# One decoder step: in the chunked recurrence, half of the heads keep their token rows in the other half of the partitions, and the products between channels and tokens are issued in turn through four quarters of TensorE

## The chip, the core and the metric

The kernel runs on one NeuronCore of one Trainium2 chip. The metric is the device time of one execution in microseconds. A core has TensorE (PE in the rows, with its weight loads apart as PEld), VectorE (DVE), ScalarE (ACT), GpSimd (POOL) and SyncE (SP), each with its own instruction stream; they wait for one another through semaphores. TensorE's results land in PSUM, which has 128 partitions and eight banks; everything else is held in SBUF, with 128 partitions too.

## The reference

One inference step of a decoder layer is computed for a prompt of 1024 tokens and for 8 samples of 4 new tokens. The layer has an input projection, an RWKV7 recurrence beside latent attention, a memory attention and a convolutional feed-forward part. Only the recurrence concerns us. For each of 8 heads a 64 x 64 state S is carried over the tokens:

```python
def step(S, inp):
    r_t, d_t, k_t, v_t, kk_t, a_t = inp
    sa = -jnp.einsum('bhvk,bhk->bhv', S, kk_t)
    S = (S * d_t[:, :, None, :] + sa[..., None] * (kk_t * a_t)[:, :, None, :]
         + v_t[..., None] * k_t[:, :, None, :])
    return S, jnp.einsum('bhvk,bhk->bhv', S, r_t)
...
state, out = lax.scan(step, state0.astype(jnp.float32), xs)
```

## The kernel before

**Layout.** The recurrence is `rwkv_chunk_stage` (from L1756). The 1024 prompt tokens are cut into 16 chunks of 64 tokens (`NCH` is 16, `CH` is 64), and a seventeenth pass does the 32 sample tokens in the same way. Eight heads are four pairs p: pair p has one head's 64 channels in partitions 0 to 63 and the other's in 64 to 127 (`HALF`). Pairs 0 and 1 form half `hf` 0, pairs 2 and 3 half 1, and each half has four PSUM banks of its own: PX, PY, PV and PU.

**Quarters.** Every matmul of this stage has a 64 x 64 float32 stationary operand. The partitions it reads decide which 64 rows of TensorE's array it uses, and the partitions of its output decide which 64 columns. Before the change a head's token rows lie in the same half of the partitions as its channels, so each product reads and writes one half: only two of the array's four quarters are used, rows 0 to 63 with columns 0 to 63 and rows 64 to 127 with columns 64 to 127. A float32 matmul appears in the trace as two MATMUL records (passes), each with a weight load. In the program a loop over `HALF` issues the two heads of a pair one after the other.

**One chunk c, in TensorE's order** (rows' names in brackets):

1. `pe_products(c)`: the products of keys and queries (rc_KR, rc_BK; L1805 with 128 moving columns, L1808), which fire `a_made` for each half, and transposes by the identity (L1816), which fire `vt_made` for each half.
2. `solution(c-1)`: L2010 and L2012 accumulate the right-hand side of the previous chunk in PU and fire `sa_made`.
3. `pe_first_level(c)`: L1830, L1832, L1834.
4. `outputs(c-1)`: state and output of the previous chunk, five products for each pair (L2022, L2024, L2026, L2028, L2030), which fire `o_made`.
5. `pe_levels(c)`: levels 1 to 5 of a triangular inverse by repeated squaring (L1847, L1850, L1853), the two halves in turn, and then L1859.

**VectorE for the same chunk:** `dve_masks(c)` (L1937, L1939, L1944 for each half, after `a_made`; the second fires `a_taken`), `dve_solution(c-1)` (L1965 for each half), `dve_state(c-1)` (L1972 twice and L1974 for each half, after `o_made`), then `dve_levels(c)` (L1955 for each level and half, which fires `t_taken`, with the operands of the next chunk, L1917 to L1928, between levels). **ScalarE** copies PY to SBUF after `vt_made` (L1881), copies the levels' results (L1890, L1893, L1895), L1905 for rc_WT (`wt_taken`), and scales the old state (L2050). Each engine runs its list in that order; a product of level n+1 waits for VectorE's `t_taken` and ScalarE's `n_taken` of level n for its half.

Of the kernel before, what the change touches and what calls it, by code (L numbers as in the profile page):

```python
# [18 lines left out]
ALU = mybir.AluOpType  # L19
# [17 lines left out]
CH = 64  # L37
NCH = TP // CH
# [93 lines left out]
class K:  # L132
# [74 lines left out]
class TokenScale:  # L207
# [4 lines left out]
    W = C3 // 4  # L212
# [1540 lines left out]
HALF = slice(0, HD), slice(HD, P)  # L1753


def rwkv_chunk_stage(k, c, b, kk, keep, free_b, free_kk, tail, mh_at):  # L1756


# [5 lines left out]
    S = {n: k.sem(f"rc_{n}") for n in (  # L1764
        "masks", "zero", "prev", "exp", "bd", "a_made", "vt_made", "a_taken", "l_taken", "vt_taken",
        "lev_made", "n_taken", "t_taken", "mv_taken", "wt_made", "wt_taken", "sa_made", "sa_taken",
        "o_made", "o_taken", "end", "s1", "s_ready", "out",
        "ut_made", "ut_taken", "m_own", "sb_in", "sx_made", "sx_taken", "ex", "ns_made", "sum", "ns_done")}
    NT_, N_, TT_ = 0, 1, 2

# [2 lines left out]
    PX, PY, PV, PU = [[k.bank[4 * hf + n] for hf in range(2)] for n in range(4)]  # L1773
    two = lambda bank, lo, w=CH: bank[:, lo:lo + 2 * w].rearrange("p (q n) -> p q n", q=2)
    at = lambda n, w=CH: slice(n, n + w)
    L_RAW, MV_, WT_, SA_, ST_, O_ = 128, 256, 384, 0, 128, 256
    ident = [k.masks[h, MK["ident"] + j * HD:MK["ident"] + (j + 1) * HD] for j, h in enumerate(HALF)]
    with ExitStack() as ctx:
        rm = k.sb(ctx, "rc_masks", [P, 2, 4, CH])
# [16 lines left out]
        def pe_products(pe, c_):  # L1796

            sl = c_ % 2
            KR, BK = KR_[:, sl], BK_[:, sl]
            pe.wait_ge(S["bd"], 5 * (c_ + 1))  # L1800
            for hf in range(2):
                for q, p in enumerate(pairs(hf)):
                    for j in range(2):
                        for h in HALF:
                            pe.matmul(PX[hf][h, at(256 * q + 128 * j, 128)], BK[h, p, j, :],  # L1805
                                      KR[h, p].rearrange("p a n -> p (a n)"), start=True, stop=True)
                    for h in HALF:
                        mm = pe.matmul(PV[hf][h, at(L_RAW + 64 * q)], KR[h, p, 0, :], BK[h, p, 0, :], start=True, stop=True)  # L1808
                mm.then_inc(S["a_made"], 1)
            for hf in range(2):  # L1810
                if c_:
                    pe.wait_ge(S["wt_taken"], 2 * (c_ - 1) + hf + 1)
                for q, p in enumerate(pairs(hf)):
                    for j in range(4):
                        for i, h in enumerate(HALF):
                            mm = pe.matmul(PY[hf][h, at(256 * q + 64 * j)], BK[h, p, j, :] if j < 3 else KR[h, p, 0, :], ident[i],  # L1816
                                           start=True, stop=True)
                mm.then_inc(S["vt_made"], 1)

        def pe_first_level(pe, c_, levels):  # L1820
            W, A4, tm = W_[:, c_ % 2], A4_[:, c_ % 2], tm_[:, c_ % 2]
# [15 lines left out]
        def pe_levels(pe, c_, levels):  # L1837
            W, tm = W_[:, c_ % 2], tm_[:, c_ % 2]
            for lev in range(1, levels):
                for hf in range(2):  # L1840
                    if lev == 1:
                        pe.wait_ge(S["mv_taken"], 2 * c_ + hf + 1)
                    pe.wait_ge(S["n_taken"], 10 * c_ + 2 * (lev - 1) + hf + 1)
                    pe.wait_ge(S["t_taken"], 12 * c_ + 2 * (lev - 1) + hf + 1)
                    for q, p in enumerate(pairs(hf)):
                        for h in HALF:
                            mm = pe.matmul(PV[hf][h, at(64 * q)], W[h, p, N_, :], W[h, p, TT_, :], start=True, stop=True)  # L1847
                        if lev < levels - 2:
                            for h in HALF:
                                pe.matmul(PY[hf][h, at(128 * q)], W[h, p, N_, :], W[h, p, NT_, :], start=True, stop=True)  # L1850
                        if lev < levels - 1:
                            for h in HALF:
                                mm = pe.matmul(PY[hf][h, at(128 * q + 64)], W[h, p, NT_, :], W[h, p, N_, :], start=True, stop=True)  # L1853
                    mm.then_inc(S["lev_made"], 1)
            for hf in range(2):
                pe.wait_ge(S["t_taken"], 12 * c_ + 2 * (levels - 1) + hf + 1)
                for q, p in enumerate(pairs(hf)):
                    for h in HALF:
                        mm = pe.matmul(PY[hf][h, at(WT_ + 64 * q)], tm[h, p, 3, :], W[h, p, TT_, :], start=True, stop=True)  # L1859
                mm.then_inc(S["wt_made"], 1)  # L1860

        def exponential(act, c_, sl, n):
# [97 lines left out]
                        scaled(dve, c_ + 1, 1 - sl, 4)  # L1960

        def dve_solution(dve, c_):
            for hf in range(2):
                dve.wait_ge(S["sa_made"], 2 * c_ + hf + 1)
                dve.tensor_scalar(SA[:, 2 * hf:2 * hf + 2, :], two(PU[hf], SA_), -1.0, None, ALU.mult).then_inc(S["sa_taken"], 1)  # L1965

        def dve_state(dve, c_):
            dve.wait_ge(S["s1"], 4 * (c_ + 1))
            for hf in range(2):
                dve.wait_ge(S["o_made"], 2 * c_ + hf + 1)  # L1970
                for q, p in enumerate(pairs(hf)):
                    dve.scalar_tensor_tensor(St[:, p, :], PU[hf][:, at(ST_ + 64 * q)], end[:, p, :], S1[:, p, :],  # L1972
                                             ALU.mult, ALU.add).then_inc(S["s_ready"], 1)
                dve.tensor_copy(c[:, 2 * hf:2 * hf + 2, bass.ds(1 + c_ * CH, CH)], two(PU[hf], O_)).then_inc(S["o_taken"], 1)  # L1974

        with nc.Block() as block:
            @block.sync
# [22 lines left out]
            @block.tensor  # L2000
            def _(pe):
                def solution(c_):
                    W, MV, WT = W_[:, c_ % 2], MV_t[:, c_ % 2], WT_t[:, c_ % 2]
                    pe.wait_ge(S["s_ready"], 4 * (c_ + 1))
                    pe.wait_ge(S["o_taken"], 2 * (c_ + 1))
                    for hf in range(2):
                        pe.wait_ge(S["wt_taken"], 2 * c_ + hf + 1)
                        for q, p in enumerate(pairs(hf)):
                            for h in HALF:
                                pe.matmul(PU[hf][h, at(SA_ + 64 * q)], W[h, p, TT_, :], MV[h, p, :], start=True, stop=False)  # L2010
                            for h in HALF:
                                mm = pe.matmul(PU[hf][h, at(SA_ + 64 * q)], WT[h, p, :], St[h, p, :], start=False, stop=True)  # L2012
                        mm.then_inc(S["sa_made"], 1)

                def outputs(c_):
                    KR, A4, tm = KR_[:, c_ % 2], A4_[:, c_ % 2], tm_[:, c_ % 2]
                    for hf in range(2):
                        pe.wait_ge(S["sa_taken"], 2 * c_ + hf + 1)
                        for q, p in enumerate(pairs(hf)):
                            st, o = at(ST_ + 64 * q), at(O_ + 64 * q)  # L2020
                            for h in HALF:
                                pe.matmul(PU[hf][h, st], tm[h, p, 0, :], SA[h, p, :], start=True, stop=False)  # L2022
                            for h in HALF:
                                pe.matmul(PU[hf][h, st], tm[h, p, 1, :], tm[h, p, 2, :], start=False, stop=True)  # L2024
                            for h in HALF:
                                pe.matmul(PU[hf][h, o], St[h, p, :], KR[h, p, 1, :], start=True, stop=False)  # L2026
                            for h in HALF:
                                pe.matmul(PU[hf][h, o], SA[h, p, :], A4[h, p, 1, :], start=False, stop=False)  # L2028
                            for h in HALF:
                                mm = pe.matmul(PU[hf][h, o], tm[h, p, 2, :], A4[h, p, 3, :], start=False, stop=True)  # L2030
                        mm.then_inc(S["o_made"], 1)
# [1185 lines left out]
```

## Time and profile before

| | |
|---|---|
| time, median of 3 runs | 2344.28 us (2339.0 to 2347.64) |
| span of the profiled execution | 2347.7 us |
| its own time | within the span by 0.1 us: the slowest of the three runs, 2347.64 us |
| PE busy, share of the span | 2198.9 us, 94% |
| DVE / ACT / POOL busy | 57% / 28% / 5% |
| the 16 chunks of the recurrence | from 786.5 to 1052.7 us; one chunk takes 16.13 us |

The busy times are those of the whole span; a busy PE in the profile is one with a matmul in flight, and the length that a row gives for a matmul includes its way through the array. How fast matmuls follow one another is read from the starts of successive rows.

### The profile page before, as it was taken

The numbers are of one execution on the slowest core, as the hardware profiler recorded it, in microseconds if no ns is written. First come the engines' busy times: TensorE is split into PE (matmuls) and PEld (weight loads), VectorE is DVE, ScalarE is ACT, GpSimd is POOL, SyncE is SP. The second block draws the span as 40 slices with busy tenths as digits, with TensorE's granted clock in tenths as the row PEclk, the third lists the DMA queues.
The fourth block names the chain that finished last, engine by engine and source line by source line (L and its number), as shares of the span: only waits on it lengthen the run. The fifth ranks groups of instructions, "written<-read, shape, count | busy, mean of one in ns | idle before, by whom it ended". The sixth has DMA issues, their size and how long they took to land. (4 is left out here: it accounts for less than half of the span.)

```text
span 2347.7 us, 51172 instructions
## 1 busy us (share of the span) xinstructions
PE 2198.9 (94%) x20986; PEld 2036.9 (87%) x20986; DVE 1333.4 (57%) x2616; ACT 666.3 (28%) x1349; POOL 118.5 (5%) x194
## 2 busy tenths in 40 slices
PE   7999999987879799997999998989999999999997
PEld 6999777766668799985899988989999999999997
DVE  6357555553355455553673164456666666666676
ACT  5120244433342344431131142222221112221121
POOL 0000100005300111110000000000000000000000
PEclk9999999998978999997999999999999999999998
DMA  4111100007523100004112153011111011111012
GB/s 156 45 46 46 39 12 12 7 1 195 145 84 97 34 4 4 4 11 128 32 41 81 37 198 106 28 61 46 55 55 46 28 46 46 55 54 46 28 52 75
DMA packets 81830, 134.03 MB, mean 57 GB/s; under 512 B 27186, under 2 KB 57779, under 8 KB 81491
## 3 DMA queue, kind: packets, MB, share of 16 engines
q1 hardware_dynamic: 70482, 119.22, 15.7%
q0 software_dynamic: 4224, 8.13, 1.4%
q10 hardware_dynamic: 6912, 3.54, 0.6%
q8 instruction: 172, 2.82, 0.5%
q14 instruction: 40, 0.32, 0.0%
HBM read 121.58 MB, written 9.29 MB: 56 GB/s over the span
## 5 line engine op out<-in xcount | busy, mean ns | idle before, releaser
L280 PE MATMUL psum<-high,ff_up 128*128 128x352 f32 x2112 | 516.9, 326 | 5.1 <-DVE ff_u L2907 2.9
L280 PEld LDWEIGHTS psum<-high,ff_up 128*128 128x128 f32 x2112 | 370.4, 189 | 6.9 <-DVE ff_u L2907 3.8
L280 PE MATMUL psum<-low,ff_up 128*128 128x352 f32 x1056 | 341.1, 323 | 0.0
L443 PE MATMUL psum<-h_high,pj_part 128*128 128x352 f32 x960 | 242.0, 330 | 14.8 <-DVE h_low L550 14.7
L280 PE MATMUL psum<-hid,ff_down 128*128 128x352 f32 x1440 | 234.4, 324 | 0.8 <-DVE x L2952 0.8
L280 PEld LDWEIGHTS psum<-hid,ff_down 128*128 128x128 f32 x1440 | 232.8, 188 | 1.1 <-DVE x L2952 1.1
L280 PEld LDWEIGHTS psum<-low,ff_up 128*128 128x128 f32 x1056 | 199.4, 189 | 0.0
L2952 DVE TENSOR_TENSOR x<-x,psum 128x352 f32<-128x352 f32 x264 | 136.3, 520 | 105.6 <-PE psum L280 105.4
L443 PEld LDWEIGHTS psum<-h_high,pj_part 128*128 128x128 f32 x960 | 171.6, 191 | 20.4 <-issue 10.5
L2797 ACT ACTIVATE ff_up<-ff_slot 128x1024 fp32r<-128x1024 f32 x46 | 48.3, 1051 | 391.0 <-PE psum L280 384.7
L443 PE MATMUL psum<-h_low,pj_part 128*128 128x352 f32 x480 | 157.2, 327 | 0.0
L2832 ACT ACTIVATE ff_c<-ff_u,vecs 128x1072 f32<-128x1072 f32 x44 | 56.6, 1285 | 156.0 <-DVE ff_u L2907 119.4
L280 PE MATMUL psum<-m_high,mq_part 128*128 128x352 f32 x384 | 94.7, 327 | 5.3 <-PEq L156 5.3
L280 PE MATMUL psum<-m_high,mo_part 128*128 128x352 f32 x384 | 94.3, 327 | 2.6 <-PEq L2509 2.6
L443 PEld LDWEIGHTS psum<-h_low,pj_part 128*128 128x128 f32 x480 | 91.5, 191 | 1.0
L1847 PE MATMUL psum<-rc_W 64*64 64x64 f32 x1296 | 89.5, 222 | 1.6 <-DVE rc_W L1955 0.4
L799 PE MATMUL psum<-mp_kT,mp_qT 96*128 96x512 f32 (+2 forms) x192 | 76.2, 507 | 0.0
L1853 PE MATMUL psum<-rc_W 64*64 64x64 f32 x1024 | 73.4, 218 | 0.3 <-issue 0.3
L280 PEld LDWEIGHTS psum<-m_high,mq_part 128*128 128x128 f32 x384 | 67.9, 191 | 5.5 <-issue 5.5
L819 PE MATMUL psum<-mp_v,mp_pT 128*128 128x64 f32 x576 | 71.4, 269 | 0.5 <-DVE acc L987 0.5
L1847 PEld LDWEIGHTS psum<-rc_W 64*64 64x64 f32 x1296 | 65.7, 134 | 6.3 <-ACT rc_W L1893 2.7
L280 PEld LDWEIGHTS psum<-m_high,mo_part 128*128 128x128 f32 x384 | 67.9, 191 | 2.8 <-issue 2.8
(434 smaller groups left out, 4341.3 us busy)
## 6 DMA issues: line engine op xcount, KB each, us to landing
ff_slot<-in_w_up SPq DMA_DIRECT2D x44, 512.0 KB, 3.6
ff_slot<-in_w_down SPq DMA_DIRECT2D x22, 512.0 KB, 3.6
pj_slot<-in_w_in SPq DMA_DIRECT2D x20, 512.0 KB, 3.6
mk_slot<-in_w_mkv SPq DMA_DIRECT2D x16, 512.0 KB, 3.9
mz_k<-in_memk SPq DMA_DIRECT2D x8, 1024.0 KB, 5.6
mz_v<-in_memv SPq DMA_DIRECT2D x8, 1024.0 KB, 7.7
ms_keys<-in_lat SPq DMA_DIRECT2D x56, 128.0 KB, 2.9
ms_keys<-in_lat POOLq DMA_DIRECT2D x48, 128.0 KB, 3.1
```

The source lines that it names most:

```text
L280: mm = pe.matmul(ps, w(a, kk), rhs(b, kk), start=(kk == 0 and n == 0), stop=(kk == nk - 1 and n == 2))
L443: mm = pe.matmul(ps, part[:, j, a, kk * P:(kk + 1) * P], third((H, L)[b][:, kk, :], n), start=(kk == 0 and i == 0), stop=(kk == DK - 1 and ...
L799: mm = pe.matmul(B[2 * (i % 2) + c // 512][:, 0:w], qT[0:QH, j, i * P:(i + 1) * P], kT[h % 3][0:QH, c:c + w], start=True, stop=True)
L819: mm = pe.matmul(B[6][:, 0:HD], pT[:, i % 2, t * P:(t + 1) * P], v[:, t, h * HD:(h + 1) * HD], start=(t == 0), stop=(t == i))
L1847: mm = pe.matmul(PV[hf][h, at(64 * q)], W[h, p, N_, :], W[h, p, TT_, :], start=True, stop=True)
L1853: mm = pe.matmul(PY[hf][h, at(128 * q + 64)], W[h, p, NT_, :], W[h, p, N_, :], start=True, stop=True)
L2797: act.activation(dst[:, 0], slot[:, j], ACT.Copy).then_inc(S["w_high"], 1)
L2832: act.activation(cv[:, j, :], u[:, j, 2:U], ACT.Identity, bias=k.vecs[:, bass.ds(b0, 1)], scale=k.vecs[:, bass.ds(w2, 1)]).then_inc(S["c_f ...
L2952: dve.tensor_tensor(xs, xs, B[4 + g % 4][:, 0:C3], ALU.add).then_inc(S["down_taken"], 1)
```

## The change

Half 1 (pairs 2 and 3) of the 16 prompt chunks keeps its channels where they were but puts its token rows in the opposite half of the partitions (`tokens` returns `HALF` reversed). A product from channels to tokens or from tokens to channels of half 1 then uses the two other quarters of the array. Products from tokens to tokens (the levels) stay in the same two quarters for both halves. The loops over the half are moved inside, so that four successive matmuls of the mixed products go to four different quarters.

Two quarters that share columns write the same PSUM partitions, so they are kept in different banks. Where a sum of half 1 mixes products of both kinds (the right-hand side of the solution, and the output), it is now made in two banks, PU[1] and PX[1], and VectorE adds the two with one more instruction (semaphores `sa_first`, `o_first`). As PX[1] is in use until VectorE has masked the products of chunk c, `solution(c-1)` now waits for `a_taken` of both halves of chunk c after its first four matmuls. Several waits for one half are now waits for both. The seventeenth pass keeps the old layout but has the new order of issue in `pe_products`.

```diff
+def tokens(c_, hf):
+    return HALF[::-1] if hf and c_ < NCH else HALF
...
+    SA2_, O2_ = 0, 128
...
             pe.wait_ge(S["bd"], 5 * (c_ + 1))
-            for hf in range(2):
-                for q, p in enumerate(pairs(hf)):
-                    for j in range(2):
-                        for h in HALF:
-                            pe.matmul(PX[hf][h, at(256 * q + 128 * j, 128)], BK[h, p, j, :],
...
-                mm.then_inc(S["a_made"], 1)
...
+            if 2 <= c_ < NCH:
+                pe.wait_ge(S["o_taken"], 2 * c_)
+            for q in range(2):
+                for j in range(2):
+                    for hf in range(2):
+                        p = 2 * hf + q
+                        for h, t in zip(HALF, tokens(c_, hf)):
+                            pe.matmul(PX[hf][t, at(256 * q + 128 * j, 128)], BK[h, p, j, :],
                                       KR[h, p].rearrange("p a n -> p (a n)"), start=True, stop=True)
...
+                for hf in range(2):
+                    p = 2 * hf + q
+                    for h, t in zip(HALF, tokens(c_, hf)):
+                        mm = pe.matmul(PV[hf][t, at(L_RAW + 64 * q)], KR[h, p, 0, :], BK[h, p, 0, :], start=True, stop=True)
+                    if q:
+                        mm.then_inc(S["a_made"], 1)
+            if c_:
+                pe.wait_ge(S["wt_taken"], 2 * c_)
+            for q in range(2):
+                for j in range(4):
+                    for hf in range(2):
...
+                        if q and j == 3:
+                            mm.then_inc(S["vt_made"], 1)
...
         def dve_solution(dve, c_):
...
+            dve.wait_ge(S["sa_made"], 2 * c_ + 2)
+            dve.tensor_scalar(SA[:, 2:4, :], two(PU[1], SA_), -1.0, None, ALU.mult).then_inc(S["sa_first"], 1)
+            dve.wait_ge(S["sa_first"], c_ + 1)
+            dve.tensor_tensor(SA[:, 2:4, :], SA[:, 2:4, :], two(PX[1], SA2_), ALU.subtract).then_inc(S["sa_taken"], 1)
...
+                dve.tensor_copy(out, two(PU[hf], O_)).then_inc(S["o_first"] if hf else S["o_taken"], 1)
+                if hf:
+                    dve.wait_ge(S["o_first"], c_ + 1)
+                    dve.tensor_tensor(out, out, two(PX[hf], O2_), ALU.add).then_inc(S["o_taken"], 1)
...
+                    pe.wait_ge(S["wt_taken"], 2 * c_ + 2)
+                    inverse = lambda hf, q, t: pe.matmul(PU[hf][t, at(SA_ + 64 * q)], W[t, 2 * hf + q, TT_, :], MV[t, 2 * hf + q, :],
+                                                         start=True, stop=(hf == 1))
+                    for q in range(2):
+                        for t in tokens(c_, 1):
+                            inverse(1, q, t)
+                    pe.wait_ge(S["a_taken"], 2 * min(c_ + 2, NCH))
+                    for q in range(2):
+                        for t in tokens(c_, 0):
+                            inverse(0, q, t)
+                        for hf in (0, 1) if q else (1, 0):
+                            p = 2 * hf + q
+                            out = PX[hf][:, at(SA2_ + 64 * q)] if hf else PU[hf][:, at(SA_ + 64 * q)]
+                            for h, t in zip(HALF, tokens(c_, hf)):
+                                mm = pe.matmul(out[t, :], WT[h, p, :], St[h, p, :], start=(hf == 1), stop=True)
+                            if q:
+                                mm.then_inc(S["sa_made"], 1)
...
                 def outputs(c_):
...
+                    pe.wait_ge(S["sa_taken"], 2 * c_ + 2)
+                    for q in range(2):
+                        st, o = at(ST_ + 64 * q), at(O_ + 64 * q)
+                        each = [(hf, 2 * hf + q, h, t) for hf in range(2) for h, t in zip(HALF, tokens(c_, hf))]
+                        for hf, p, h, t in each:
+                            pe.matmul(PU[hf][h, st], tm[t, p, 0, :], SA[t, p, :], start=True, stop=False)
+                        for hf, p, h, t in each:
+                            pe.matmul(PU[hf][h, st], tm[t, p, 1, :], tm[t, p, 2, :], start=False, stop=True)
+                        for hf, p, h, t in each:
+                            out = PX[hf][h, at(O2_ + 64 * q)] if hf else PU[hf][h, o]
+                            pe.matmul(out, St[h, p, :], KR[h, p, 1, :], start=True, stop=(hf == 1))
+                        for hf, p, h, t in each:
+                            pe.matmul(PU[hf][h, o], SA[t, p, :], A4[t, p, 1, :], start=(hf == 1), stop=False)
+                        for hf in range(2):
+                            p = 2 * hf + q
+                            for h, t in zip(HALF, tokens(c_, hf)):
+                                mm = pe.matmul(PU[hf][h, o], tm[t, p, 2, :], A4[t, p, 3, :], start=False, stop=True)
+                            if q:
+                                mm.then_inc(S["o_made"], 1)
```

On TensorE, from the start of a chunk to the first level, before (one pair after the other; the pattern of the first two rows comes four times, that of the next two four times, that of L2010 and L2012 four times):

```order
L1805 MATMUL psum<-rc_KR,rc_BK 64x128 x4
L1808 MATMUL psum<-rc_BK,rc_KR 64x64 x2
...
L1816 MATMUL psum<-masks,rc_BK 64x64 x6
L1816 MATMUL psum<-masks,rc_KR 64x64 x2
...
L2010 MATMUL psum<-rc_MV,rc_W 64x64 x2
L2012 MATMUL psum<-rc_S,rc_WT 64x64 x2
```

The same place of the changed program, whose lines L1814, L1819, L1829, L2028 and L2041 are the former L1805, L1808, L1816, L2010 and L2012 (the first two rows come twice, the next two twice):

```order
L1814 MATMUL psum<-rc_KR,rc_BK 64x128 x8
L1819 MATMUL psum<-rc_BK,rc_KR 64x64 x4
...
L1829 MATMUL psum<-masks,rc_BK 64x64 x12
L1829 MATMUL psum<-masks,rc_KR 64x64 x4
...
L2028 MATMUL psum<-rc_MV,rc_W 64x64 x6
L2041 MATMUL psum<-rc_S,rc_WT 64x64 x4
L2028 MATMUL psum<-rc_MV,rc_W 64x64 x2
L2041 MATMUL psum<-rc_S,rc_WT 64x64 x4
```

The number of matmuls is the same; each run of equal products is now twice as long, because the two halves stand side by side in it. The new wait for `a_taken` stands after the fourth of the six L2028.

On VectorE, from the solution to the first of the levels, before:

```order
L1965 TENSOR_SCALAR rc_SA<-psum 128x128
...
L1972 SCALAR_TENSOR_TENSOR rc_S<-psum,rc_end,rc_S_10133 128x64 x2
L1974 ISA
L1974 COPY y<-psum 128x2x64
...
L1955 TENSOR_TENSOR rc_W<-rc_W,psum 128x2x64
```

And in the changed program, where L1978 and L1980 are the former L1965 of either half, L1989 and L1992 the former L1972 and L1974, and L1969 the former L1955:

```order
L1978 TENSOR_SCALAR rc_SA<-psum 128x128
L1979 REGISTER_ALU
L1980 TENSOR_SCALAR rc_SA<-psum 128x128
L1982 TENSOR_TENSOR rc_SA<-rc_SA,psum 128x128
...
L1992 COPY y<-psum 128x2x64
L1995 TENSOR_TENSOR y<-y,psum 128x2x64
...
L1969 TENSOR_TENSOR rc_W<-rc_W,psum 128x2x64
```

Two instructions are added, L1982 in the solution and L1995 at the end of the state, both ahead of the levels' L1969 on the same engine.

## Rows read from the trace of the kernel before

**Rows 1.** The page: busy time, share of the span and instructions of each engine.
```profile
PE 2198.9 (94%) x20986; PEld 2036.9 (87%) x20986; DVE 1333.4 (57%) x2616; ACT 666.3 (28%) x1349; POOL 118.5 (5%) x194
```

**Rows 2.** Stretches: length, busy time of each engine, then granted clock, DMA share, GB/s.
```profile
850.68:866.81 16.13, 15.75 (x486) 15.33 (x484) 9.11 (x30) 7.66 (x25) 2.74 (x4) 1.00 0.02 4
...
755.60:782.80 27.20, 20.61 (x156) 16.73 (x156) 13.31 (x19) 8.53 (x15) 0.32 (x1) 1.00 0.17 59
782.90:789.70 6.80, 3.17 (x36) 3.21 (x38) 3.04 (x9) 0.42 (x1) 0.00 (x0) 0.50 0.11 39
```

**Rows 3.** TensorE's instructions in order of time, chunk from 850.68: start, length, what.
```profile
850.68 0.60 PE L1805 MATMUL psum<-rc_KR,rc_BK 64*64 64x128 f32 x8
...
852.89 0.52 PE L1816 MATMUL psum<-masks,rc_BK 64*64 64x64 f32 x12
...
854.76 0.28 PE L2010 MATMUL psum<-rc_MV,rc_W 64*64 64x64 f32 x4
...
855.70 0.28 PE L1830 MATMUL psum<-rc_A,rc_W 64*64 64x64 f32 x4
...
857.10 0.28 PE L2022 MATMUL psum<-rc_SA,rc_tm 64*64 64x64 f32 x4
...
859.43 0.28 PE L1847 MATMUL psum<-rc_W 64*64 64x64 f32 x4
...
860.87 0.33 PE L1847 MATMUL psum<-rc_W 64*64 64x64 f32 x4
...
866.30 0.68 PE L1859 MATMUL psum<-rc_W,rc_tm 64*64 64x64 f32 x16 [0.33 <-DVE rc_W L1955]
```

**Rows 4.** VectorE's instructions in order of time, the same chunk.
```profile
852.00 0.29 DVE L1937 TENSOR_TENSOR rc_W<-psum,rc_masks 128x128 f32<-128x128 f32 x1 [1.36 <-PE psum L1808]
852.21 0.68 DVE L1939 TENSOR_TENSOR rc_A<-psum,rc_masks 128x512 f32<-128x512 f32 x1
852.93 0.29 DVE L1944 SCALAR_TENSOR_TENSOR rc_W<-rc_A,rc_masks 128x128 f32<-128x128 f32 x1
...
853.34 0.68 DVE L1939 TENSOR_TENSOR rc_A<-psum,rc_masks 128x512 f32<-128x512 f32 x1
...
855.91 0.29 DVE L1965 TENSOR_SCALAR rc_SA<-psum 128x128 f32<-128x128 f32 x1 [0.18 <-PE psum L2012]
858.56 0.48 DVE L1972 SCALAR_TENSOR_TENSOR rc_S<-psum,rc_end,rc_S 128x64 f32<-128x64 f32 x2 [2.36 <-PE psum L2030]
858.95 0.28 DVE L1974 COPY y<-psum 128x128 f32 x1
...
860.04 0.28 DVE L1974 COPY y<-psum 128x128 f32 x1
860.44 0.29 DVE L1955 TENSOR_TENSOR rc_W<-rc_W,psum 128x128 f32<-128x128 f32 x1
```

**Rows 5.** ScalarE's instructions in order of time, the same chunk.
```profile
854.98 0.60 ACT L1881 ACTIVATE rc_tm<-psum 128x512 f32<-128x512 f32 x1 [0.34 <-PE psum L1816]
...
857.31 0.38 ACT L1890 ACTIVATE rc_W<-psum 128x256 f32<-128x256 f32 x1
```

**Rows 6.** TensorE in order of time elsewhere: whole array, then four column strips.
```profile
545.27 0.49 PE L1116 MATMUL psum<-masks,ms_keys 128*128 128x128 f32 x3
545.60 0.27 PE L1126 MATMUL psum<-masks,ms_kr 128*128 128x128 f32 x1
545.80 0.64 PE L1139 MATMUL psum<-ms_kT,qabs 128*32 128x128 f32 x16
546.26 0.40 PE L1142 MATMUL psum<-ms_krT,ms_qd 128*32 128x128 f32 x8
```

**Rows 7.** TensorE in order of time elsewhere: two row halves over all columns.
```profile
668.07 0.79 PE L1433 MATMUL psum<-rw,rp_w 64*128 64x352 f32 x1
668.08 0.79 PE L1437 MATMUL psum<-rw,rp_w 64*128 64x352 f32 x1
668.66 0.79 PE L1433 MATMUL psum<-rw,rp_w 64*128 64x352 f32 x1
```

More of the change, by code:

```diff
@@ L1766, in rwkv_chunk_stage @@
         "lev_made", "n_taken", "t_taken", "mv_taken", "wt_made", "wt_taken", "sa_made", "sa_taken",
-        "o_made", "o_taken", "end", "s1", "s_ready", "out",
+        "o_made", "o_taken", "sa_first", "o_first", "end", "s1", "s_ready", "out",
         "ut_made", "ut_taken", "m_own", "sb_in", "sx_made", "sx_taken", "ex", "ns_made", "sum", "ns_done")}
@@ L1810, in pe_products @@
[L1810 to L1816, printed above, removed]
+            if 2 <= c_ < NCH:
[6 more added lines that the diff above has]
+                            pe.matmul(PX[hf][t, at(256 * q + 128 * j, 128)], BK[h, p, j, :],
+                                      KR[h, p].rearrange("p a n -> p (a n)"), start=True, stop=True)
+                for hf in range(2):
[4 more added lines that the diff above has]
+                        mm.then_inc(S["a_made"], 1)
@@ L1817, in pe_products @@
+            if c_:
[4 more added lines that the diff above has]
+                        p = 2 * hf + q
+                        for i, (h, t) in enumerate(zip(HALF, tokens(c_, hf))):
+                            mm = pe.matmul(PY[hf][t, at(256 * q + 64 * j)], BK[h, p, j, :] if j < 3 else KR[h, p, 0, :], ident[i],
                                            start=True, stop=True)
-                mm.then_inc(S["vt_made"], 1)
+                        if q and j == 3:
+                            mm.then_inc(S["vt_made"], 1)
@@ L1857, in pe_levels @@
                 for q, p in enumerate(pairs(hf)):
-                    for h in HALF:
-                        mm = pe.matmul(PY[hf][h, at(WT_ + 64 * q)], tm[h, p, 3, :], W[h, p, TT_, :], start=True, stop=True)
+                    for h, t in zip(HALF, tokens(c_, hf)):
+                        mm = pe.matmul(PY[hf][h, at(WT_ + 64 * q)], tm[t, p, 3, :], W[t, p, TT_, :], start=True, stop=True)
                 mm.then_inc(S["wt_made"], 1)
@@ L1962, in dve_solution @@
         def dve_solution(dve, c_):
-            for hf in range(2):
-                dve.wait_ge(S["sa_made"], 2 * c_ + hf + 1)
-                dve.tensor_scalar(SA[:, 2 * hf:2 * hf + 2, :], two(PU[hf], SA_), -1.0, None, ALU.mult).then_inc(S["sa_taken"], 1)
+            dve.wait_ge(S["sa_made"], 2 * c_ + 1)
+            dve.tensor_scalar(SA[:, 0:2, :], two(PU[0], SA_), -1.0, None, ALU.mult).then_inc(S["sa_taken"], 1)
+            dve.wait_ge(S["sa_made"], 2 * c_ + 2)
+            dve.tensor_scalar(SA[:, 2:4, :], two(PU[1], SA_), -1.0, None, ALU.mult).then_inc(S["sa_first"], 1)
+            dve.wait_ge(S["sa_first"], c_ + 1)
+            dve.tensor_tensor(SA[:, 2:4, :], SA[:, 2:4, :], two(PX[1], SA2_), ALU.subtract).then_inc(S["sa_taken"], 1)
         def dve_state(dve, c_):
@@ L1973, in dve_state @@
                                              ALU.mult, ALU.add).then_inc(S["s_ready"], 1)
-                dve.tensor_copy(c[:, 2 * hf:2 * hf + 2, bass.ds(1 + c_ * CH, CH)], two(PU[hf], O_)).then_inc(S["o_taken"], 1)
+                out = c[:, 2 * hf:2 * hf + 2, bass.ds(1 + c_ * CH, CH)]
+                dve.tensor_copy(out, two(PU[hf], O_)).then_inc(S["o_first"] if hf else S["o_taken"], 1)
+                if hf:
+                    dve.wait_ge(S["o_first"], c_ + 1)
+                    dve.tensor_tensor(out, out, two(PX[hf], O2_), ALU.add).then_inc(S["o_taken"], 1)
         with nc.Block() as block:
@@ L2005, in solution @@
                     pe.wait_ge(S["o_taken"], 2 * (c_ + 1))
[L2006 to L2013, printed above, removed]
+                    pe.wait_ge(S["wt_taken"], 2 * c_ + 2)
@@ L2015, in outputs @@
                 def outputs(c_):
                     KR, A4, tm = KR_[:, c_ % 2], A4_[:, c_ % 2], tm_[:, c_ % 2]
[L2017 to L2031, printed above, removed]
+                    pe.wait_ge(S["sa_taken"], 2 * c_ + 2)
@@ new lines, in outputs @@
+                    for q in range(2):
[11 more added lines that the diff above has]
+                        for hf in range(2):
+                            p = 2 * hf + q
+                            for h, t in zip(HALF, tokens(c_, hf)):
+                                mm = pe.matmul(PU[hf][h, o], tm[t, p, 2, :], A4[t, p, 3, :], start=False, stop=True)
+                            if q:
+                                mm.then_inc(S["o_made"], 1)
```

2 lines of the change are left out of this document (removed).

## Prediction

> **What bounds the kernel now.** I read the page first: TensorE has a matmul in flight for 94% of the span, the other engines for 57% at most [rows 1]. Then the stretches: in one chunk of the recurrence PE is busy for 15.75 of 16.13 us at the full clock, VectorE for 9.11, ScalarE for 7.66 [rows 2]. Last the instructions in order of time [rows 3 to 5]. There the reader is to see that TensorE goes from group to group without a gap, and that the one long wait is at the chunk's end, where L1859 waits for VectorE. So the chunk is bound by the rate at which TensorE takes 64-wide passes. With 16 chunks the recurrence is about 258 of 2348 us; a chunk that is 1 us shorter is worth 0.7%.
>
> **The rates.** Two quarters together: 48 passes of the first level from 855.70 to 857.10 are 1.40 us, 0.117 us for four passes, 0.029 each. With 128 moving columns: 852.89 - 850.68 = 2.21 us, less 16 passes of L1808 at 0.029, leaves 1.74 us for 32 passes of L1805, 0.055 each, nearly twice as long [rows 3].
>
> No row of this stage has four quarters in use. Elsewhere the parts are there. Sixteen passes in four column strips that share all 128 rows start from 545.80 to 546.26, 0.029 each with 128 moving columns; on the whole array (L1116) a pass of that width takes 0.11, as three of them end 0.49 after the first start and a single one lasts 0.27 [rows 6]. So four column strips run at once. Two row halves that share all columns start 0.01 us apart and both have their next pass about 0.59 later: they run at once too [rows 7]. The quarters added share rows with one old quarter and columns with the other, and each kind of sharing runs at full rate in these rows. I take four at once: four passes of 64 columns in 0.058 instead of 0.117, eight of 128 in 0.22 instead of 0.44. The other bound is no gain at all, the two-quarter rates; both ends are kept below.
>
> The Trainium skill, "TensorE: Matmul & The Clock Gate", section "The mechanism" of Part 3, says that a weight load overlaps matmuls in flight only when the row group differs. Two quarters on the same rows would then take turns, and the sum would be that of the second rival below. The column strips do not agree: they share all rows, and their passes, each with a load, still step 0.029.
>
> **The change, on a clock that starts with the chunk (850.68).** *Before*: products end at 2.21, transposes at 4.08, solution at 5.02, first level at 6.42, outputs at 8.75, level 2 starts at 10.19 (860.87), the next chunk at 16.13 [rows 2, 3]. *After*:
>
> 1. Products: 1.74/2 + 0.47/2 = 1.11. VectorE began its masks at 1.32, after half 0's products, which ended at 1.11 of the 2.21; now both halves end at 1.11. So the masks stay where they are, and the second mask of L1939 ends at 853.34 + 0.68, that is 3.34 [rows 4].
> 2. Transposes, 64 passes: 1.87/2 = 0.93, end 2.04. Both fire at the end; ScalarE's two copies of 0.60 [rows 5] end by 2.04 + 0.21 + 1.2 = 3.45, before the first level wants them.
> 3. Solution: the first four matmuls use two quarters (0.23) and end at 2.28. Then comes the new wait for the masks of half 1: 3.34, and 0.14 to wake PE (L1955 ends 860.73, level 2 starts 860.87), so 3.48. That is a wait of 1.2 us where there was none. Of the other twelve matmuls eight are on the old two quarters: four turns of 0.117, 0.47, end 3.95.
> 4. First level, unchanged, 1.40: ends 5.35. Meanwhile VectorE negates both halves and subtracts: start 3.95 + 0.21 (855.70 to 855.91), second negation 0.20 later, 0.29 long, subtraction 0.04 behind its end (as L1944 behind L1939) and again about 0.29 (L1955 reads the same shape): 4.98, 5.1 with the wake-up. Hidden by the first level with 0.2 to spare; without that cover it would cost 0.33.
> 5. Outputs: of five products four go to four quarters; the third (L2026) has both halves on the old two. Six turns instead of ten: 2.33 x 0.6 = 1.40, end 6.75.
> 6. State: VectorE starts 0.30 after the outputs (857.10 + 1.17 = 858.26 to 858.56). Both halves are now ready at once: two L1972 and L1974 start 0.39 apart in all and L1974 is followed after 0.20, so half 0 from 7.05, half 1 from 7.64, its copy 8.03 to 8.31, the added L1995 8.35 to 8.64. Behind it on VectorE is level 1's L1955, 0.20 to 0.40 later (860.04 to 860.44 is 0.40): 8.55 to 8.75, done 8.84 to 9.04.
> 7. Level 1 on PE: 6.75 to 8.15; ScalarE's copies are done long before (L1890 now near 5.5). Level 2 must wait for that L1955: 8.98 to 9.18 instead of 10.19. This second new wait is 0.8 to 1.0 us.
> 8. From level 2 on nothing is changed, nor is the wait at L1859, as VectorE still makes the next operands there.
>
> So TensorE's own work falls by 0.88 + 0.23 + 0.93 + 0.23 + 0.93 = 3.2 us a chunk, but two thirds come back as waits for VectorE, and the chunk is 1.01 to 1.21 shorter: 15.0 us. I take 1.11, the middle, since both spacings occur [rows 4]. Fifteen chunks have all these parts: 16.7 us. The first chunk has only the products and gains at most as much as one other. The seventeenth pass fires `a_made` of half 0 only with half 1, so its masks (1.13 a half, 852.21 to 853.34) start up to 1.1 later, and the tail after the last chunk has two more VectorE instructions (0.6). I let these cancel, with 2 us on either side. The profiled execution, 2347.7, becomes 2331.0; it stands 3.4 us above the median of the runs, so against the median the forecast is 2344.3 - 16.7 = **2327.6 us**.
>
> **Rivals.**
>
> *Slower: four quarters run no faster than two.* Then the waits stay without the gain. Both halves' products end at 2.21, so the masks start at 2.42 and the last needed one ends at 2.42 + 1.34 (852.00 to 853.34) + 0.68 = 4.44; the rest of the solution (0.70) starts at 4.58, first level ends 6.68, outputs 9.01, state from 9.31, L1955 ends 11.10 to 11.30, level 2 starts 11.24 to 11.44: 1.05 to 1.25 later, 15 times, and 1 or 2 us at the ends: 2344 + 18 = 2362. It decides from the point where four passes of mixed products take over about 0.087 us, midway between 0.058 and 0.117. Against it stand the strips and the row halves [rows 6, 7]; for it, that no row has quarters differing in rows and columns together at four.
>
> *Same: passes are issued no faster than 0.029 each,* which is the shortest step in any of these rows, whether two quarters or four strips. The 128-column products then still halve (0.055 to 0.029), the 64-column ones don't. Products end 1.39, masks 3.62, solution 4.46, first level 5.86, outputs 8.19, state from 8.49, level 2 at 10.42 to 10.62: 0.33 later, 15 times, 2344 + 5 = 2349. For it: no shorter sustained step is seen; against it: the strips have 128 moving columns, so 0.029 is a quarter of the array's own 0.11 there, and the array explains it alone.
>
> *The clock falls.* PE will wait some 2.5 us of 15. The clock was full over 27.2 us with PE busy for 20.61 (76%), and half over 6.8 us with 3.17 (47%) [rows 2]; the changed chunk is above 80%, so I expect full clock. Every us at the lower clock costs up to half a us of matmul work, so some 2.3 us of it in each chunk eat the gain: about 2344.
>
> **How the numbers follow.** Forecast 0.80, slower rival 0.08, issue-bound 0.07, clock 0.05. The three runs spread over 0.4%, so 0.5% (12 us) is about what a measurement can tell from no change. The forecast's own range is 1.0 to 1.3 us a chunk with 2 us at the ends and 4 for the runs, 2317 to 2336; it holds most of its 0.80. To have 8 in 10 the range goes up into the issue-bound and clock cases: 2315 to 2346. Faster by over 0.5% means below 2332.6: about 0.85 of the forecast, 0.68. Slower is the first rival and some of the other two, 0.11. Same is the rest, 0.21.
>
> **What would show it.** Eight passes of L1814 in about 0.22 and sixteen of L1829 in about 0.23; VectorE's masks still at 1.32 in the chunk; a PE wait of about 1.2 us at L2028 for L1953 and one of 0.8 to 1.0 at level 2 for L1969; chunks 15.0 us apart at full clock. I would be wrong if sixteen passes of L1829 still take 0.47, if level 2 does not wait for VectorE, or if the clock column shows a half inside the recurrence.

## The result, and the profile after

The changed kernel takes 2330.73 us (median of 4 runs, 2326.64 to 2335.08), the kernel before 2343.34 (4 runs, 2339.0 to 2347.64). The ratio is 0.994, with a 95% interval of 0.9922 to 0.9957: 12.6 us less, against a forecast of 2327.6. The profiled execution took 2326.64 us with a span of 2325.0.

From the start of the first chunk to that of the seventeenth pass the traces show 250.6 us instead of 266.2, 15.6 less (forecast 16.7). The other 7 us between the two spans lie ahead of the recurrence, which began at 779.2 us instead of 786.5, in code that the change doesn't touch (in the eight other runs below it began anywhere from 778.4 to 785.5). I don't count them.

The page of the changed kernel, its line of busy times, answers to [rows 1]:

```profile
PE 2148.7 (92%) x20986; PEld 1981.4 (85%) x20986; DVE 1332.4 (57%) x2648; ACT 664.0 (29%) x1349; POOL 118.3 (5%) x194
```

Two chunks as stretches (length, busy time of PE, PEld, DVE, ACT and POOL, then granted clock, DMA share, GB/s) answer to [rows 2]:

```profile
868.87:883.73 14.86, 13.01 (x490) 12.32 (x486) 9.35 (x32) 7.52 (x24) 2.75 (x4) 1.00 0.02 4
914.01:929.45 15.44, 12.89 (x490) 12.22 (x487) 9.38 (x33) 7.63 (x24) 2.76 (x4) 1.00 0.02 4
782.20:1027.90 245.70, 208.58 (x7612) 195.78 (x7605) 147.50 (x510) 121.25 (x384) 44.37 (x64) 1.00 0.02 4
```

TensorE is busy for 13.0 us of a chunk instead of 15.75, and its clock stays full. But the chunks are no longer equal: 14.86 and 15.44 here, 14.76 to 15.97 from the second chunk to the fifteenth, where all but two were 16.13; their mean (chunks 2 to 15) is 15.22 instead of 16.23. TensorE in order of time, the chunk from 868.87, answers to [rows 3]:

```profile
869.00 0.53 PE L1814 MATMUL psum<-rc_KR,rc_BK 64*64 64x128 f32 x12
...
870.61 0.50 PE L1829 MATMUL psum<-masks,rc_BK 64*64 64x64 f32 x20
...
871.11 0.40 PE L2028 MATMUL psum<-rc_MV,rc_W 64*64 64x64 f32 x7
872.34 0.27 PE L2028 MATMUL psum<-rc_MV,rc_W 64*64 64x64 f32 x2 [0.83 <-DVE rc_A L1953]
...
872.85 0.28 PE L1844 MATMUL psum<-rc_A,rc_W 64*64 64x64 f32 x4
...
874.25 0.28 PE L2052 MATMUL psum<-rc_SA,rc_tm 64*64 64x64 f32 x5
...
875.65 0.28 PE L1861 MATMUL psum<-rc_W 64*64 64x64 f32 x4
...
876.70 0.28 PE L1861 MATMUL psum<-rc_W 64*64 64x64 f32 x3
877.31 0.21 PE L1861 MATMUL psum<-rc_W 64*64 64x64 f32 x1 [0.33 <-issue]
...
877.88 0.33 PE L1861 MATMUL psum<-rc_W 64*64 64x64 f32 x4
...
883.40 0.53 PE L1873 MATMUL psum<-rc_W,rc_tm 64*64 64x64 f32 x12 [0.33 <-DVE rc_W L1969]
883.73 0.33 PE L1814 MATMUL psum<-rc_KR,rc_BK 64*64 64x128 f32 x2
```

The reader is to see the new wait at L2028 for the masks, then a gap-free run to 876.70, and there something that no row of before prepared for: TensorE stands still for 0.55 us between two starts, in the middle of four equal passes, with "issue" as the releaser, which means that the profile shows nothing that it waited for. The last two rows are the chunk's end (L1873 is the former L1859) and the start of the next. VectorE in the same chunk answers to [rows 4]; the two added instructions are L1982 and L1995:

```profile
870.27 0.29 DVE L1951 TENSOR_TENSOR rc_W<-psum,rc_masks 128x128 f32<-128x128 f32 x1 [1.25 <-PE psum L1819]
...
871.60 0.68 DVE L1953 TENSOR_TENSOR rc_A<-psum,rc_masks 128x512 f32<-128x512 f32 x1
...
873.59 0.29 DVE L1982 TENSOR_TENSOR rc_SA<-rc_SA,psum 128x128 f32<-128x128 f32 x1
875.95 0.48 DVE L1989 SCALAR_TENSOR_TENSOR rc_S<-psum,rc_end,rc_S 128x64 f32<-128x64 f32 x2 [2.07 <-PE psum L2063]
...
877.24 0.29 DVE L1995 TENSOR_TENSOR y<-y,psum 128x128 f32 x1
877.44 0.29 DVE L1969 TENSOR_TENSOR rc_W<-rc_W,psum 128x128 f32<-128x128 f32 x1
```

Last, TensorE's waits from 800 to 1000 us (what waited, for what: us in total, times, longest):

```profile
PE psum L2028 <- DVE rc_A L1953: 8.6, 12, 1.0
PE psum L1861 <- DVE rc_W L1969: 8.2, 22, 0.7
PE psum L1873 <- DVE rc_W L1969: 4.3, 13, 0.6
PE psum L1829 <- issue: 1.8, 5, 0.5
PE psum L1861 <- issue: 1.5, 4, 0.4
PE psum L2059 <- issue: 1.5, 3, 0.7
PE psum L1864 <- issue: 0.9, 1, 0.9
```

The first two are the forecast's two new waits. The rows with "issue" are 15 pauses on several lines; in the same stretch of before there is one, at L1853. In the view of DMA queues for that stretch one row will matter below, that of the instruction packets (packets, MB, share of 16 engines):

```profile
q8 instruction: 50, 0.82, 1.7%
```

### The profile page after: what moved, and what is told of

Same layout as the page of the kernel before. It is cut to its first block and busy times, and to the rows that moved or that the text cites. A ratio compares the mean times of both kernels' runs of the same rounds, so it can differ in the third digit from the quotient of the medians.

```text
span 2325.0 us, 51218 instructions
## 1 busy us (share of the span) xinstructions
PE 2148.7 (92%) x20986; PEld 1981.4 (85%) x20986; DVE 1332.4 (57%) x2648; ACT 664.0 (29%) x1349; POOL 118.3 (5%) x194
## 3 DMA queue, kind: packets, MB, share of 16 engines
q1 hardware_dynamic: 70482, 119.22, 15.6%
## 5 line engine op out<-in xcount | busy, mean ns | idle before, releaser
L1861 PE MATMUL psum<-rc_W 64*64 64x64 f32 x1296 | 92.6, 223 | 10.7 <-DVE rc_W L1969 8.7
L1867 PE MATMUL psum<-rc_W 64*64 64x64 f32 x1024 | 75.3, 218 | 1.1 <-issue 1.0
L1904 ACT ACTIVATE rc_W<-psum 128x256 f32<-128x256 f32 x128 | 49.2, 385 | 75.0 <-PE psum L1867 62.2
```

What stands on the lines that cost most here:

```text
L1904: act.activation(W[:, pp, 0:2, :].rearrange("p q a n -> p q (a n)"), two(PY[hf], 0, 128), ACT.Copy)\
```

## The experiments

### Two quarters, everything else kept

```diff
 def tokens(c_, hf):
-    return HALF[::-1] if hf and c_ < NCH else HALF
+    return HALF
```

> The changed kernel with the token rows of half 1 left where they were: the same instructions in the same order with all the new waits and the two added VectorE instructions, but only two quarters in use. Theory (four quarters run at once, and that is the gain): the rates fall back to those of two quarters, products end 2.2 us into the chunk, level 2 starts at 11.2 to 11.4, a chunk takes 17.1 to 17.4 us and the kernel about 2362. Rival (the gain comes from the order of issue and the merged waits, the quarters add nothing): a chunk stays at 15.2 us, about 2331. On the unexplained pauses of TensorE (gaps of 0.3 to 1.1 us at matmuls that wait for no semaphore, 22 in the recurrence of the changed kernel, one before): if they come from instructions being taken faster than they are delivered, they go away here, at most 2; if they come from the new waits or the order, about 20 stay.

Measured: 2359.07 us (2358.2 to 2359.66), ratio 1.0057 (1.004 to 1.0074): slower than before. A chunk takes 17.01 us in the mean, and there is one pause of the unexplained kind instead of 24 (at most 2, if instructions are taken faster than they are delivered, was the forecast). TensorE and then VectorE in order of time, chunk from 869.03:

```profile
869.03 1.04 PE L1814 MATMUL psum<-rc_KR,rc_BK 64*64 64x128 f32 x16
...
871.24 0.87 PE L1829 MATMUL psum<-masks,rc_BK 64*64 64x64 f32 x24
```

```profile
879.57 0.48 DVE L1969 TENSOR_TENSOR rc_W<-rc_W,psum 128x128 f32<-128x128 f32 x2
```

Two such groups of products with their L1819 take 2.2 us, and the transposes 1.87, the rates of [rows 3]. So the quarters are what gains: 17.01 - 15.22 = 1.8 us a chunk. The new order of issue, the waits and the added VectorE instructions that they need cost 17.01 - 16.23 = 0.8. That has the sign of my slower rival, whose price (18 us) was 5 too high: TensorE hardly waits at L2028 (about 0.1 us; VectorE's masks end at 4.32 and not at 4.44), and level 2, after VectorE's first add at level 1 (879.57 + 0.29), starts 10.97 us into the chunk and not at 11.24 to 11.44.

### Four quarters, the halves issued one after the other

```diff
-            for q in range(2):
-                for j in range(2):
-                    for hf in range(2):
-                        p = 2 * hf + q
+            for hf in range(2):
+                for q in range(2):
+                    p = 2 * hf + q
+                    for j in range(2):
...
-                    for q in range(2):
+                    for hf_, q in ((0, 0), (0, 1), (1, 0), (1, 1)):
```

The transposes and the solution's sums are turned in the same way.

> The changed kernel with its layout of four quarters, but each mixed product is issued for all of half 0 and then for all of half 1, as before. Theory (only matmuls that follow one another directly into different quarters overlap): the rates are those of two quarters, half 0 of the products ends at 1.1 us and the masks are never late, level 2 starts near 10.4 because of the added instruction on VectorE, a chunk takes 16.2 to 16.5 us, the kernel 2345 to 2350. Rival (the quarters overlap by layout, whatever the order of issue): a chunk of 15.2 us, about 2331.

Measured: 2329.61 us (2324.39 to 2332.4), ratio 0.9924 (0.9907 to 0.994), a chunk of 15.25 us: the same as the changed kernel. My expectation fell, for two reasons that the trace shows. TensorE in order of time, chunk from 829.07 (L1826 is the former L1829 here, L2024 the former L2028):

```profile
829.64 0.70 PE L1814 MATMUL psum<-rc_KR,rc_BK 64*64 64x128 f32 x12
...
830.74 0.27 PE L1826 MATMUL psum<-masks,rc_BK 64*64 64x64 f32 x2
830.84 0.28 PE L1814 MATMUL psum<-rc_KR,rc_BK 64*64 64x128 f32 x2
...
831.26 0.52 PE L1826 MATMUL psum<-masks,rc_BK 64*64 64x64 f32 x14
...
832.43 0.40 PE L2024 MATMUL psum<-rc_MV,rc_W 64*64 64x64 f32 x7
```

VectorE in the same chunk (L1949 and L1965 are the former L1953 and L1969):

```profile
831.77 0.68 DVE L1949 TENSOR_TENSOR rc_A<-psum,rc_masks 128x512 f32<-128x512 f32 x1
...
837.60 0.70 DVE L1965 TENSOR_TENSOR rc_W<-rc_W,psum 128x128 f32<-128x128 f32 x2
```

Within one half the passes do run at the two quarters' 0.029 (14 of L1826 from 831.26 to 831.67). But the last products of half 1 run beside the first transposes of half 0, which the program issues behind them: L1826 starts at 830.74, the last row of L1814 at 830.84. This is why the solution is reached 3.4 us into the chunk and not at 4.1. And at 3.4 it meets the end of VectorE's second mask (L1949, 831.77 + 0.68), which came then in the changed kernel too (871.60 + 0.68): TensorE had gained the time in the first part only to wait there. Level 1's add starts at 8.53 as against 8.57. So the order in turn is not needed for the gain; the layout is, and VectorE's chain from the masks on sets the pace up to level 2 (8.97 us into the chunk against 9.01).

### Without the wait for the masks

```diff
-    SA2_, O2_ = 0, 128
+    SA2_, O2_ = 256, 128
...
-                    pe.wait_ge(S["a_taken"], 2 * min(c_ + 2, NCH))
+                    pe.wait_ge(S["l_taken"], min(2 * c_ + 3, 2 * NCH))
...
-                            out = PX[hf][:, at(SA2_ + 64 * q)] if hf else PU[hf][:, at(SA_ + 64 * q)]
+                            out = PV[0][:, at(SA2_ + 64 * q)] if hf else PU[hf][:, at(SA_ + 64 * q)]
```

> The changed kernel with half 1's second sum of the solution in free columns of bank PV[0] instead of PX[1]: the solution's wait for the masks of both halves of the next chunk becomes one for the first mask of half 0, which is over by then. Theory (that wait is on the path, with VectorE's masks as the next bound): the wait of 1.0 to 1.2 us is gone, VectorE starts the solution's negations 0.5 us earlier right behind its masks, outputs start 0.5 to 0.65 us earlier, a chunk is 0.4 to 0.65 us shorter, the kernel 5 to 10 us below the changed one, 2321 to 2326. Rival (the wait is hidden by VectorE's chain from masks to the subtraction): below 0.15 us a chunk, 2329 to 2331.

Measured: 2332.26 us (2328.68 to 2337.26), ratio 0.9937 (0.9921 to 0.9954). Nothing was gained, and the chunk is longer, 15.58. Yet the wait is gone and the cause is not the rival's, VectorE's chain. VectorE, and then TensorE, in the chunk from 860.64:

```profile
864.30 0.28 DVE L1978 TENSOR_SCALAR rc_SA<-psum 128x128 f32<-128x128 f32 x1
```

```profile
864.86 0.33 PE L1846 MATMUL psum<-rc_W,rc_A 64*64 64x64 f32 x4 [0.46 <-issue]
...
868.61 0.27 PE L1861 MATMUL psum<-rc_W 64*64 64x64 f32 x1 [0.74 <-issue]
...
873.18 0.33 PE L1867 MATMUL psum<-rc_W 64*64 64x64 f32 x4 [0.61 <-issue]
```

VectorE starts the negations 3.66 us into the chunk instead of 4.20, half a us earlier, as forecast. Then TensorE pauses three times without a releaser. In all there are 37 such pauses, 28.8 us, where the changed kernel has 24 with 12.9.

### VectorE's output copies behind the levels' adds

```diff
+                if before and lev <= 2:
+                    dve_output(dve, c_ - 1, lev == 2)
                 if ahead and lev <= 4:
                     scaled(dve, c_ + 1, 1 - sl, lev - 1)
```

`dve_output` holds the two copies (level 1) or the added sum (level 2), taken out of `dve_state`.

> The changed kernel with VectorE's two output copies moved behind level 1's adds, and the added sum of the output behind level 2's. Theory (these three instructions stand on the path in front of level 1's add and so of level 2): level 2 starts 0.5 to 0.75 us earlier, the wait of 0.66 us there nearly goes, VectorE has idle time between the later levels for the moved work, and a chunk is 0.3 to 0.7 us shorter: 4 to 10 us less than the changed kernel, 2320 to 2327. Rival (VectorE is as late at the end of the chunk, where the next products wait for its operands, so the time comes back as a longer wait there): within 2 us of the changed kernel.

Measured: 2328.77 us (2327.65 to 2333.19), ratio 0.9926 (0.991 to 0.9943), a chunk of 15.31 us: no change against the changed kernel. TensorE's waits from 800 to 1000 us (L2035 is the former L2028):

```profile
PE psum L2035 <- DVE rc_A L1953: 7.1, 11, 1.0
PE psum L1873 <- DVE rc_W L1969: 3.7, 11, 0.5
PE psum L1864 <- issue: 3.3, 5, 0.9
PE psum L1829 <- issue: 2.7, 6, 0.9
PE psum L1861 <- DVE rc_W L1969: 2.5, 11, 0.3
```

The wait at level 2 fell from 8.2 to 2.5 us, as meant, and the wait at the chunk's end (L1873) fell too, so the rival is wrong in its cause, though its number (within 2 us) came out. The time came back as pauses: 30, 18.5 us.

### A second theory: TensorE's instructions arrive too slowly

So whatever wait was taken away, pauses took its place. I numbered all records of TensorE's instructions (weight loads, passes, waits) in order of time and took each pause of over 0.25 us at an instruction that waits for no semaphore, from the first chunk to the seventeenth pass. The mean is that of chunks 2 to 15; the last four rows are the runs that follow.

```
kernel           instructions  mean chunk  pauses     number       at successive    shortest
                 in a chunk        us      n   us    modulo 256    packets: mean us     us
before               973         16.23     1   0.6      193              -               -
changed              974         15.22    24  12.9      193            3.95            3.61
two quarters         974         17.01     1   0.4      193              -               -
halves in turn       974         15.25    15   8.2      193            4.03            3.91
no mask wait         974         15.58    37  28.8      193            4.03            3.45
outputs later        974         15.31    30  18.5      193            3.95            3.36
both waits out       974         15.36    44  34.6      193            4.03            3.36
padded              1022         16.57    52  41.3      193            4.09            3.30
lean                 910         15.05     8   4.7      193            4.39            3.94
both and lean        910         14.20    27  20.1      193            3.81            3.54
```

All 239 pauses, in ten programs and on many lines, stand at an instruction whose number leaves 193 when divided by 256. An instruction packet in the DMA records has 16384 bytes, which with 256 instructions to a packet is 64 bytes for each. The Trainium skill, "Perfetto Trace Analysis", section "The 4-stage abstract model", gives the same 64 bytes. Every pause ends 1.18 to 1.61 us after a packet of queue q8 has landed, and where there is no pause, the instruction at such a place never starts sooner than 1.20 us after one (605 places in all, ten programs). Where TensorE pauses at two successive packets, these are 3.3 to 5.2 us apart, about 4.0 in the mean. A chunk has 974 instructions, 3.8 packets: at 4.0 us each that is 15.2 us. Before, a packet lasted 16.13 / 3.8 = 4.24 us. By this theory (delivery) the kernel had 6% of room, the change used it up, and nothing but fewer instructions helps from here on. Four runs tested it.

**Padded:** 48 instructions more, where TensorE waits anyway.

```diff
+                    for n in range(12):
+                        pe.matmul(PU[1][HALF[n % 2], at(384 + 64 * (n // 6))], ident[n % 2], ident[n % 2], start=True, stop=True)
                     pe.wait_ge(S["a_taken"], 2 * min(c_ + 2, NCH))
```

> The changed kernel with twelve float32 matmuls without use (48 instructions of TensorE, results in free columns of PU[1]) put where TensorE waits 0.7 to 1.2 us in each solution for VectorE's masks; they take 24 passes at 0.029, 0.70 us, and fit into that wait. Theory (delivery): in every kernel so far the pauses without a wait stand exactly 256 TensorE instructions apart (or a multiple), 256 instructions of 64 bytes are one 16 KB instruction packet, and two pauses at successive packets are 3.4 to 5.0 us apart, 3.95 in the mean. A chunk of 974 instructions is 3.8 packets and cannot be much shorter than 15.0 us. With 1022 it is 3.99 packets: a chunk 0.6 to 0.8 us longer, 9 to 12 us in all, about 2341, with more pauses. Rival (engine time and semaphores set the chunk, the pauses are an accident of some matmuls): the pads are hidden in the wait, a chunk within 0.15 us of 15.2, about 2331 to 2333.

Measured: 2349.55 us (2345.98 to 2354.11), ratio 1.0017 (1.0007 to 1.0027), a chunk of 16.57 us. TensorE's waits from 800 to 1000 us begin with

```profile
PE psum L1829 <- issue: 7.5, 12, 1.0
PE psum L1873 <- DVE rc_W L1969: 4.2, 12, 0.6
PE psum L1867 <- issue: 4.1, 6, 1.1
```

The wait for the masks that should have hidden the pads is gone from the list, and the pads cost 1.35 us a chunk, not at most 0.15: the rival falls; even unhidden they would cost 0.70. The theory's 0.6 to 0.8 is too low as well; at four packets to a chunk the pauses fall at nearly the same place in each chunk and 52 of them stand, at 4.09 us a packet (16.3 us a chunk).

**Lean:** 64 instructions fewer, ahead of the same wait (it leaves work out).

```diff
-                for j in range(4):
+                for j in range(2 if 0 < c_ < NCH else 0, 4):
```

> The changed kernel without the transposes of the first two operands (rc_BK 0 and 1) in chunks 1 to 15: 16 matmuls, 64 instructions of TensorE a chunk less; the products that read these transposes still run, on old data. The transposes left out lie ahead of the solution's wait for VectorE's masks, so by engine time they are hidden. Theory (delivery): 910 instructions are 3.55 packets, 14.0 us at 3.95; the chunk falls to what waits and engines allow, which the changed kernel's chunks without a pause show as 14.76: 0.3 to 0.5 us a chunk, 5 to 7 us below the changed kernel, about 2324, with few pauses left. Rival (engine time and waits): the wait for the masks only grows by 0.5 us, and the chunk stays within 0.1 us of 15.2, 2329 to 2332.

Measured: 2326.28 us (2324.13 to 2327.02), ratio 0.9918 (0.9902 to 0.9935), a chunk of 15.05 us, seven of fourteen between 14.76 and 14.83. Its waits in that stretch:

```profile
PE psum L2028 <- DVE rc_A L1953: 16.5, 13, 1.5
...
PE psum L1829 <- issue: 1.4, 2, 0.7
```

The pauses fell to 8 and the wait for the masks doubled. The gain, 4.5 us on the medians, lies between the theory's 5 to 7 and the rival's 2 at most, and so does the chunk, 0.17 shorter where the theory had 0.3 to 0.5 and the rival 0.1 at most; the pauses side with the theory, the time alone would not settle it.

**Both waits out:** the two edits above on one kernel, with the copy of rc_BK and two more operands of the next chunk made in VectorE's idle time ahead of the outputs.

```diff
+                    for n in (0, 2, 3):
+                        scaled(dve, c_ + 1, 1 - sl, n)
                     if before:
                         dve_state(dve, c_ - 1)
```

> The changed kernel with the solution's second sum in PV[0] (no wait for all masks), VectorE's output copies behind level 1 and the added sum behind level 2, and three of the next chunk's operands made in VectorE's idle time ahead of the outputs. By waits and engines alone a chunk loses 0.5 us at the solution, 0.5 to 0.7 at level 2 and some tenths at its end. Rival (waits and engines bind): a chunk of 13.3 to 14.0 us, the kernel 2305 to 2315. Theory (delivery): the same 974 instructions need 3.8 packets, so the time taken out comes back as pauses at every packet: a chunk of 15.0 to 15.6 us, 2328 to 2334, with more pauses than the 24 of the changed kernel, most of them 256 instructions apart.

Measured: 2328.22 us (2322.84 to 2333.3), ratio 0.992 (0.9901 to 0.9939), a chunk of 15.36 us and 44 pauses. Its waits from 800 to 1000 us:

```profile
PE psum L1829 <- issue: 5.2, 8, 1.4
PE psum L1861 <- issue: 4.1, 7, 1.0
PE psum L1861 <- DVE rc_W L1969: 2.6, 13, 0.2
```

The waits for VectorE fell from 21.1 us in that stretch to 2.6, and the chunk is as long as it was without these edits. Only delivery had forecast that.

**Both and lean:** the same with 64 instructions fewer, by the edit of the lean kernel.

> The kernel with both waits taken out and VectorE's work moved, and with the 64 instructions a chunk less (the transposes of rc_BK 0 and 1 left out in chunks 1 to 15; the products that read them run on old data). Theory (delivery): 3.55 packets at 3.95, a chunk of 13.9 to 14.5 us, 0.8 to 1.2 us below the kernel with the same waits and all instructions: 2312 to 2320. Rival (waits and engines bind in both): the transposes stand on TensorE's path now, so 0.5 us a chunk less than that kernel at the most.

Measured: 2314.15 us (2312.98 to 2315.08), ratio 0.9868 (0.9852 to 0.9885), a chunk of 14.20 us, 1.16 below the last kernel where engine time would have allowed 0.5. A chunk of 3.55 packets at 4.0 is 14.2. This one leaves work out too and is no version to use. Of the kernels with all the work, none beats the changed one by more than these intervals can tell.

## Why the prediction was right, point by point

- **Four quarters at once** (steps 1, 2 and 5): right. Products end 1.12 us into the chunk (1.11 forecast), transposes take 1.03 instead of 1.87 (0.93 forecast), the outputs 1.40. The run with two quarters prices it at 1.8 us a chunk. The Trainium skill's rule ("TensorE: Matmul & The Clock Gate", "The mechanism"), by which a load overlaps only across row groups, does not hold here: quarters on the same rows overlapped, as the strips of [rows 6] had said. The reading of [rows 7] lacks its clock, which was 0.50 there: 352 columns at the whole array's 0.11 for 128 would take 0.30 at full clock and 0.60 at half, so two row halves every 0.59 do run at once, as I had it.
- **The first new wait** (step 3): right, L2028 goes on at 3.47 (3.48), the solution ends at 3.98 (3.95).
- **The cover for the negations** (step 4): right, L2052 follows the first level without a wait.
- **State, the added sum, level 2** (steps 6 and 7): right, L1989 at 7.08 (7.05), L1995 at 8.37 (8.35), L1969 at 8.57 (8.55 to 8.75), level 2 at 9.01 (8.98 to 9.18).
- **"From level 2 on nothing is changed"** (step 8): wrong in both directions. In the one chunk of these without a pause (from 808.24) level 2 to the next chunk takes 5.75 us and not 5.94, which gives 14.76 us. The step that I left out is L1859, now L1873: it goes between token rows and channels, so the change moves its half 1 to the other quarters too. From its first pass to the next chunk it takes 0.33 us (883.40 to 883.73) instead of 0.51 (866.30 to 866.81, [rows 2, 3]); with two quarters it was 0.52 again. The pauses, a term that the sum doesn't have, then bring the mean to 15.22, 0.46 more. I had 15.0: the two errors cancel in part, and 0.2 us a chunk, 3 us in all, is left.
- **The ends**: the first chunk gained 1.8 us, more than the 1.1 that I had called its most, and the last chunk, up to the seventeenth pass, takes 0.4 longer; within the 2 us allowed. So the recurrence is only 1.1 us off a forecast of 16.7, in part by luck: the first chunk's 1.8 and two longer chunks of before (16.99 and 16.73, a mean of 16.23 and not 16.13) make up for much of it.
- **Rivals.** The clock case is out: 1.00 from 782 to 1028 us; the 0.50 that follows begins 1.9 us ahead of the seventeenth pass. The issue-bound rival had the right number at the wrong scale. Passes do step faster than 0.029 (64 transposes in 1.03 us are 0.016), but over a packet of 128 passes 3.3 to 4.0 us are 0.026 to 0.031 a pass. It is a bound on the average, which bites where a stretch of fast passes reaches the end of a packet.

## What to carry to other kernels

When small matmuls get faster, count TensorE's instructions: a float32 matmul is four of them here, and 256 need some 4 us to arrive. If the chunk is near that, a wait removed comes back as "issue" pauses, and only fewer instructions make it shorter. Before pricing a faster unit, ask which wait its time will run into: here TensorE's busy time fell by 2.7 us a chunk and the chunk by 1.0, the rest went to VectorE's masks and adds and to delivery, and setting the halves side by side in the order of issue bought nothing beyond the layout.

## What was not expected of the hardware

Instruction packets of 16 KB are fetched all through the run (50 in 200 us), each takes 0.9 to 1.6 us to move, and a pause always comes at the same place of the stream, 193 past a multiple of 256 instructions in these ten programs. No instruction at such a place, with a pause or without, started sooner than 1.18 us after a packet had landed. Why no two packets in the recurrence start less than 3.2 us apart, and no two pauses end less than 3.3, stays open: after a pause the next transfer starts 1.0 to 3.0 us later, and what triggers it was not tried.
